# Inverse levels 2 to 16 on 32x32 diagonal tiles, with regrouped late attention halves, narrow gates and a reordered entry, pooling and head

## What is computed

```python
h = rms_norm(x, mix_norm[l]); proj = h @ w_in[l]
# A: dilated windowed attention, 4 heads x 64, rotary        (q, k, v, 256 columns each)
# B: trailing means over 2, 4, 8, 16 positions, minus itself (256 columns)
# C: gated DeltaNet, 4 heads x 128, chunks                    (q, k, v, z, and 8 gate columns)
x = x + concat(A, B, C) @ w_out[l]
```

```python
A = where(strict, (kb @ kc.T) * decay, 0)
T = triangular_solve(eye + A, eye, lower=True)     # the inverse
u = T @ vb;  w = T @ (kb * exp(g))                 # then a scan over the chunks
```

## Time and profile before

| | us |
|---|---|
| median of 3 runs | 1066.82 (1066.77 to 1066.97) |
| the profiled execution | 1069.16 |
| its span, first to last instruction | 1067.4 |

### The profile page before, as it was taken

The page is one execution under the profiler, slowest core; times in us unless marked ns, Lnnn a source line. Parts: engine busy times, 40 slices in busy tenths (PEclk is TensorE's granted clock), DMA queues, the critical chain, the costliest instruction groups (busy, mean ns, idle before and its releaser), DMA issues.

```text
span 1067.4 us, 18495 instructions
## 1 busy us (share of the span) xinstructions
PE 1040.5 (97%) x6251; PEld 905.6 (85%) x6251; DVE 743.0 (70%) x1188; ACT 608.9 (57%) x1066; POOL 228.0 (21%) x257
## 2 busy tenths in 40 slices
PE   6999999999999999999999999999999999999997
PEld 5888888999987888888888888888989778888885
DVE  5766666788856866666686666669887766666665
ACT  5655555667544655555575555557665455555554
POOL 2311111097400221111122111112004003111111
PEclk9999999999999999999999999999999999999999
DMA  8866665674113476666647666665732036666661
GB/s 262 251 198 180 196 190 167 172 204 155 60 60 99 132 220 182 195 195 181 196 129 221 182 194 195 182 195 140 197 124 95 3 117 201 194 193 191 187 196 39
DMA packets 252040, 177.97 MB, mean 167 GB/s; under 512 B 5892, under 2 KB 237593, under 8 KB 251865
## 3 DMA queue, kind: packets, MB, share of 16 engines
q1 hardware_dynamic: 250880, 175.40, 55.7%
q0 software_dynamic: 432, 1.48, 0.4%
q10 hardware_dynamic: 680, 0.46, 0.1%
HBM read 176.26 MB, written 1.05 MB: 166 GB/s over the span
## 4 chain that ended last, share of the span: by engine, by line
PE 87%; DVE 5%; ACT 4%; issue 2%; POOL 1%; DMA 1%; DVEq 0%; ACTq 0%; POOLq 0%
PE bank L679 27%; PE bank L682 14%; PE bank L661 12%; PE bank L662 12%; PE bank L663 12%; DVE Wl L1716 1%; PE bank L1028 1%; PE bank L1017 1%; ACT Wh L1279 1%; PE bank L688 1%; DVE X L1748 1%; DVE xr L1920 1%; ACT X L1345 1%; PE bank L968 1%; PE bank L919 1%
## 5 line engine op out<-in xcount | busy, mean ns | idle before, releaser
L1716 DVE TENSOR_TENSOR Wl<-raw,Wh 128x1024 fp32r<-128x1024 f32 x330 | 423.0, 1288 | 84.2 <-ACT Wh L1279 83.8
L1279 ACT ACTIVATE Wh<-raw 128x1024 fp32r<-128x1024 f32 x330 | 337.5, 1053 | 77.2 <-PE bank L663 76.8
L679 PE MATMUL bank<-X,Wh 128*128 128x512 f32 x1344 | 334.7, 391 | 0.0
L679 PEld LDWEIGHTS bank<-X,Wh 128*128 128x128 f32 x1344 | 246.7, 188 | 47.6
L576 POOL TENSOR_TENSOR gact<-gact,pooled 128x256 f32<-128x256 f32 x88 | 79.2, 900 | 613.2 <-DVE gact L1804 462.3
L682 PEld LDWEIGHTS bank<-X,Wl 128*128 128x128 f32 x1344 | 183.0, 190 | 14.0 <-DVE Wl L1716 1.2
L682 PE MATMUL bank<-X,Wl 128*128 128x256 f32 x1344 | 187.8, 283 | 0.0
L661 PE MATMUL bank<-Wh,aH 128*128 128x512 f32 x336 | 132.4, 394 | 1.4 <-DVE aL L1825 1.4
L662 PE MATMUL bank<-Wl,aH 128*128 128x512 f32 x336 | 131.8, 392 | 0.0
L663 PE MATMUL bank<-Wh,aL 128*128 128x512 f32 x336 | 130.8, 389 | 0.0
L1381 ACT ACTIVATE dec<-bank 128x256 f32<-128x256 f32 x88 | 33.6, 382 | 121.7 <-PE bank L682 121.6
(11 more groups left out here) (270 smaller groups left out, 1302.5 us busy)
## 6 DMA issues: line engine op xcount, KB each, us to landing
raw<-in_ffn_w_gate SPq DMA_DIRECT2D x88, 512.0 KB, 4.0
raw<-in_ffn_w_up SPq DMA_DIRECT2D x88, 512.0 KB, 3.7
raw<-in_ffn_w_down SPq DMA_DIRECT2D x88, 512.0 KB, 4.4
raw<-in_w_in SPq DMA_DIRECT2D x50, 512.0 KB, 4.1
raw<-in_w_out SPq DMA_DIRECT2D x16, 512.0 KB, 3.3
cst<-in_consts POOLq DMA_DIRECT2D x1, 1280.0 KB, 6.1
xr<-in_x SPq DMA_DIRECT2D x2, 512.0 KB, 4.7
out_x<-big SPq DMA_DIRECT2D x3, 256.0 KB, 2.0
```

Source lines behind the costliest of these rows:

```text
L679: nc.tensor.matmul(b[:, :], piece(Wh, s)[:, k, :], X[:, k, :, :], start=k == 0, stop=False)
L1279: return nc.scalar.activation(Wh[:, s, :], raw[:, s, :], ACT.Copy).then_inc(hi_cast.sem, 1)
L1716: return nc.vector.tensor_tensor(Wl[:, s, :], raw[:, s, :], Wh[:, s, :].bitcast(F32), ALU.subtract).then_inc(lo_cast.sem, 1)
```

## The change

The levels 2 to 16 move to compact blocks: D32 and T32 hold, for each unit, the four 32x32 diagonal blocks under one another. Each level's P and D product becomes four products per unit, one per diagonal tile, with 16 columns; masks, copies and transposes shrink to a quarter. After level 16 the compact blocks are copied into Dm and DT, which GpSimd has cleared. The late attention projections are cut into groups of four (high parts) and four (low parts) records and placed between all stages. The low casts 23 to 28 move behind the levels. The gate piece has 8 columns; its product puts the weights' high and low part side by side (16 rows) against both parts of x, and small products with a comb of ones turn and add them. copy_half(2) moves ahead of the scaled copies, which also trade places with casts 6 and 7. Pooling moves ahead of the state, scores 2 and 3 ahead of the second V products, the first Xl subtraction ahead of the second normalisation. A table load moves from ahead of the V copies to behind level 4. The norm weights come over ScalarE's queue, and at the start ScalarE casts a weight piece before the splits and squares half 1 last.

```diff
...
         X0h, X0l = X0[:, :, 0, :], X0[:, :, 1, :]
         PM = sb("PM", [P, UNITS, P])
+        D32 = sb("D32", [P, UNITS, BLOCK])
...
-        gate_cols = gact[:, 0, :]
+        gate_cols = gact[0:2 * GATES, :, :]
+        gate_raw = raw[:, MIX_SLOTS[POS_GATES], 0:KT * GATES].rearrange("p (k c) -> p k c", k=KT)
...
+                pool.wait_ge(*gates_proj.at(layer, 1))
+                nc.gpsimd.memset(Dm[0:BLOCK, :, BLOCK:HALF], 0.0)
+                nc.gpsimd.memset(DT[:, :, :], 0.0).then_inc(cleared.sem, 1)
...
                 split(POS_GATES)
                 pe.wait_ge(*att_read.at(layer, 5))
-                s = MIX_SLOTS[POS_GATES]
                 for k in range(KT):
-                    m = three(bank[1][:, 0:SEQ], piece(Wh, s)[:, k, :], piece(Wl, s)[:, k, :], X0h[:, k, :], X0l[:, k, :],
-                              k == 0, k == KT - 1)
+                    m = nc.tensor.matmul(bank[1][0:2 * GATES, :], gate_weights[:, k, :, :], X0[:, k, :, :],
...
                         for c in range(HALVES):
-                            m = nc.tensor.transpose(bank[0][:, SEQ + c * P:SEQ + (c + 1) * P],
-                                                    gate_cols[:, c * P:(c + 1) * P], ident)
+                            for i in range(2):
+                                m = nc.tensor.matmul(bank[0][:, SEQ + c * GATES:SEQ + (c + 1) * GATES],
+                                                     gate_cols[:, i, c * P:(c + 1) * P], cst[0:2 * GATES, C_GATE:C_GATE + GATES],
+                                                     start=i == 0, stop=i == 1)
                         m.then_inc(gates_in.sem, 1)
...
-                def att_late(j):
-
+                def late_of(j):
+                    c = j % 2
+                    s0, s1 = MIX_SLOTS[POS_LATE], MIX_SLOTS[POS_LATE + 1]
+                    return (bank[ATT_BANKS[j]][:, 0:2 * P].rearrange("p (s c) -> p s c", s=2),
+                            slice(c * P, (c + 1) * P), slice(s0, s1 + 1, s1 - s0))
+
+                def late_high(j, ks):
+
+                    out, t, pair = late_of(j)
+                    pe.wait_ge(*hi_cast.at(layer, MIX_BASE + POS_LATE + 2))
+                    pe.wait_ge(*z_act.at(layer, j - ATT_EARLY + 3))
+                    for k in ks:
+                        w = Wh[:, pair, k * P:(k + 1) * P]
+                        nc.tensor.matmul(out, Xh[:, k, t], w, start=k == 0, stop=False)
+                        nc.tensor.matmul(out, Xl[:, k, t], w, start=False, stop=False)
+
+                def late_low(j, ks):
+
+                    out, t, pair = late_of(j)
                     split(POS_LATE + 1)
-                    pe.wait_ge(*z_act.at(layer, j - ATT_EARLY + 3))
-                    att_part(layer, j, range(KT)).then_inc(att_in.sem, 1)
+                    for k in ks:
+                        m = nc.tensor.matmul(out, Xh[:, k, t], Wl[:, pair, k * P:(k + 1) * P], start=False, stop=k == KT - 1)
+                    return m
...
-                        even = Dm[:, u, :].rearrange("p (n a s) -> p n a s", a=2, s=LEVELS[n])[:, :, 0, :]
-                        m = nc.tensor.matmul(bank[4 + c][:, h * EVEN:(h + 1) * EVEN], LT[:, u, :], even, start=True, stop=True)
+                        for q in QUARTERS:
+                            even = D32[q, u, :].rearrange("p (n a s) -> p n a s", a=2, s=LEVELS[n])[:, :, 0, :]
+                            m = nc.tensor.matmul(bank[4 + c][q, h * EVEN:(h + 1) * EVEN], LT[q, u, q], even,
+                                                 start=True, stop=True)
...
                     for h, u in units(c):
-                        m = nc.tensor.matmul(bank[6 + c][:, h * EVEN:(h + 1) * EVEN], DT[:, u, :], PM[:, u, 0:EVEN],
-                                             start=True, stop=True)
+                        for q in QUARTERS:
+                            m = nc.tensor.matmul(bank[6 + c][q, h * EVEN:(h + 1) * EVEN], T32[q, u, :], PM[q, u, 0:EVEN],
+                                                 start=True, stop=True)
                     m.then_inc(dd_done.sem, 1)
...
+                    j, k = ATT_EARLY + n // 2, 4 * (n % 2)
                     for c in range(HALVES):
                         level_p(n, c)
+                    late_high(j, range(k, k + 2))
                     for c in range(HALVES):
                         level_d(n, c)
+                    late_high(j, range(k + 2, k + 4))
                 for c in range(HALVES):
                     quarter_p(c)
-                att_late(6)
+                late_low(6, range(0, 4))
                 for c in range(HALVES):
                     quarter_d(c)
+                late_low(6, range(4, 8)).then_inc(att_in.sem, 1)
+                for c in range(HALVES):
+                    half_p(c)
+                late_low(7, range(0, 4))
+                for c in range(HALVES):
+                    half_d(c)
+                late_low(7, range(4, 8)).then_inc(att_in.sem, 1)
                 turn_qk()
-                for c in range(HALVES):
-                    half_p(c)
-                att_late(7)
-                for c in range(HALVES):
-                    half_d(c)
...
-                m.then_inc(ks_ps.sem, 1)
-                for h in range(DN_HEADS):
-                    m = nc.tensor.matmul(bank[6][:, h * P:(h + 1) * P], QK[:, h, 0, P:SEQ], St[:, h, :], start=True, stop=True)
-                m.then_inc(qs_ps.sem, 1)
-
                 pe.wait_ge(*att_read.at(layer, 8))
                 for j in range(2):
...
+                m.then_inc(qs_ps.sem, 1)
+
+                scores(2)
+                scores(3)
+
                 pe.wait_ge(*r1_done.at(layer, 1))
                 for h in range(DN_HEADS):
...
                 if first:
-                    for c, b in ROW_ORDER:
+                    for c, b in ROW_ORDER[0:2]:
                         square(c, b)
+                    hi_first(layer, 0, 0)
                     act.wait_ge(zeroed.sem, 2)
                     act.wait_ge(*turned.at(layer, 2))
-                    split(0)
-                    split(1)
-                    hi_first(layer, 0, 0)
-                    split(2)
-                    split(3)
+                    for j in range(4):
+                        split(j)
                     hi_first(layer, 0, 1)
                 else:
                     act.wait_ge(*turned.at(layer, 4 * n + 2))
...
                 hi_mix(layer, 5)
+                copy_half(2)
+                hi_mix(layer, 6)
                 scaled_high(0)
                 scaled_high(1)
-                hi_mix(layer, 6)
+                hi_mix(layer, 7)
                 scaled_high(2)
                 scaled_high(3)
-                hi_mix(layer, 7)
-                copy_half(2)
                 copy_half(3)
                 hi_mix(layer, 8)
                 hi_mix(layer, 9)
...
                         act.wait_ge(*dd_done.at(layer, 2 * n + c + 1))
-                        src = bank[6 + c][:, 0:256].rearrange("p (u n s) -> p u n s", u=4, s=s)
-                        nc.scalar.activation(blocks(Dm, c, s)[:, :, :, 0, :], src, ACT.Copy).then_inc(d_done.sem, 1)
+                        src = bank[6 + c][:, 0:4 * EVEN].rearrange("p (u n s) -> p u n s", u=4, s=s)
+                        even = D32[:, 4 * c:4 * c + 4, :].rearrange("p u (n a s) -> p u n a s", a=2, s=s)[:, :, :, 0, :]
+                        nc.scalar.activation(even, src, ACT.Copy).then_inc(d_done.sem, 1)
                     if n == 0:
                         hi_mix(layer, 28)
-                copy_half(6)
-                for c in range(HALVES):
-                    u = slice(4 * c, 4 * c + 4)
-                    src = bank[6 + c][:, 0:P].rearrange("p (u s) -> p u s", u=4)
+                    if n == 1:
+                        act.preload_act_table_set(LN_EXP)
+                act.wait_ge(*cleared.at(layer, 1))
+                act.wait_ge(*d_done.at(layer, 8))
+                nc.scalar.activation(Dm[QUARTERS[0], :, QUARTERS[0]], D32[QUARTERS[0], :, :], ACT.Copy)
+                nc.scalar.activation(Dm[QUARTERS[1], :, QUARTERS[1]], D32[QUARTERS[1], :, :],
+                                     ACT.Copy).then_inc(dm_joined.sem, 1)
+
+                def edge(c):
+                    return slice(4 * c, 4 * c + 4), bank[6 + c][:, 0:P].rearrange("p (u s) -> p u s", u=4)
+
+                for c in range(HALVES):
...
 
             act.dma_start(cst[:, 0:C_FIRST], consts[:, 0:C_FIRST]).then_inc(consts_in.sem, 16)
+            for n, weight in enumerate((ffn1_norm, mix_norm, ffn2_norm)):
+                act.dma_start(nrm_rows[n * DEPTH * KT:(n + 1) * DEPTH * KT, :],
+                              weight.rearrange("l (k c) -> (l k) c", c=P)).then_inc(norms_in.sem, 16)
...
                 small(nc.vector.scalar_tensor_tensor(gneg[:, :, 4:8], row(1), -1.0, row(1), ALU.mult, ALU.min))
+                conv_rest(9)
...
+                dve.wait_ge(*lt_done.at(layer, 2))
+                for q in QUARTERS:
```

(22 more changed lines are left out.)

163 lines of the change are left out of this document (87 added, 76 removed).

## The result

The changed kernel takes 1070.46 us (median of 7 runs, 1069.28 to 1072.04), the kernel before 1066.90 (1066.74 to 1067.39): a ratio of 1.0037, 95% interval 1.0026 to 1.0047. It is slower by 3.6 us; 23.7 us faster was forecast. The profiled executions differ by less, 1068.4 against 1067.4 us of span, because that of the kernel before took 1069.16 us, 2.3 more than its median.

A forecast was written before the change was run, and what follows sets the result against it. TensorE, busy 97% of the span, bounds the kernel. Terms -7.7 - 15.2 - 0.4 + 1.0 + 0 - 1.3 = -23.6 us, set against the 1067.4 us span, give 1043.8, against the 1066.82 median 1043.2 us; range 1034 to 1054.

The forecast's parts named there:

- Part 2: Inverse levels 2 to 16: a group on four diagonal tiles takes 0.84 us instead of 1.79; -15.2 us over 16 groups.
- Rival A: Levels 2 to 16: issue limit, step not below 16.7 ns, group 1.38 us; 1051.8 us, chance 0.07.
- C: Levels 2 to 16, rival: tiles of one bank take turns, 33 ns a record, group 2.4 us; 1068.5 us, chance 0.03.
- Rival D: Levels: small-tile bursts with waits bring 1.2 GHz from the first level until behind level 64; +39 us, 1082, chance 0.04.
- point of decision: Levels and following stages: Rival D decides once 12 us of such work per layer run at half clock.
- Part 1: Mixer entry: 2.44 us wait and 1.5 of half clock go, new wait 1.0, gate product 0.9 less; -7.7 us.
- Part 3: Between entry and inverse: GpSimd's two memsets, about 1.5 us, delay its decay-row product; +1.0 us, layer 0 only.
- Part 4: Head: moved pooling and scores cost +0.6 us per layer, the earlier Xl subtraction gives -0.6; together 0 us.
- Part 5: Start: norm weights on ScalarE's queue shorten TensorE's 2.53 us wait, root about 1 us earlier; -1.3 us.
- Cover: Levels: late attention pieces between groups hide mask waits, 0.5 us behind about 1.0 us of work; nothing taken.

The follow-up runs named there:

- e2: Changed kernel with levels 2 to 16 on two 64x64 diagonal tiles instead of four 32x32 ones; 1055.70 us, ratio 0.9898 to the kernel before.
- e7: Kernel before with VectorE's subtraction and a further 512-column transpose ahead of each level's first mask; 1085.22 us in one run (before: 1067.06).
- e4: Kernel before with VectorE's subtraction of a weight piece moved ahead of each level's first mask; 1069.23 us in one run (before: 1065.42).
- e10: Changed kernel with 64x64 tiles, copy 4 and gates copy earlier, pool products ahead of second value product, old start; 1051.95 us, ratio 0.9866 to the kernel before.
- e5: Changed kernel with the four records of each late piece between the groups issued twice; 1075.47 us (1066.14 to 1080.35 in ten runs).
- e8: Kernel before with only copy_half(2) moved, behind the cast of piece 5 instead of piece 7; 1065.82 us, ratio 0.9989.

## Why the prediction failed, point by point

**The place.** Layer 0, from the traces: entry -1.7, levels to the first scores +2.5, head +0.7, Xl subtraction -0.6, together +0.9 us; -3.8, -7.8, +0.6 and -0.6 were forecast. This is against the profiled execution of the kernel before, which is 2.3 us above its median; against the median the loss is larger.

**Part 2, the records: right.** A group's 64 records start within 0.55 us (0.53 forecast), a step of 8.7 ns; group and piece take 1.33 (1.31). Rival A, 16.7 ns, is out, and so is C, turns within a bank: four row tiles write one bank, each its own 32 partitions of it, at 8.7 ns a record. Of the two rules of the Trainium skill that the prediction weighed, the floor of about 25 ns ("TensorE: Matmul & The Clock Gate", Back-to-back issue gap) doesn't hold for tiles in turn, and the bar on row tiles in one bank ("TensorEngine Tiling (Array Packing)", Restrictions and Gotchas) shows no cost here. At full clock the stretch from levels to scores would take e2's 301.72 - 280.12 = 21.60 us less 8 x (1.72 - 1.33), 18.5 by this estimate, 7.8 less than before. That is the forecast.

**Part 2, the step that failed.** It priced a group by its records alone, with "64 x 8.2 = 0.53 us", and nothing for how the instructions reach TensorE. The groups use them faster than blocks arrive: stops of 0.59 us and 0.34 (inside the group at 288.73, 1.39 us long instead of 1.05) in layer 0, 0.34 and 1.18 in layer 1.

**Rival D, the argument against it.** "I expect no wait over 1 us there" failed in two ways. There was one of 1.18, from a source that isn't a wait in the program. And 1 us was the wrong measure: it was taken from the 2.44 us at entry, a stage of 256-column products, while in the levels 0.60 is enough (e7). The rival itself is what happened, with two corrections: the clock fell behind the first stops and not at the first level, 6 us into the levels (7 in layer 1, in the stop of 1.18), and it cost less than +39, because records at half clock don't all take twice as long (a cycle of 2.13 against 1.33). Layer 0: 28.87 - 0.93 of stops - 18.5 = 9.4 us up to the scores, 0.5 in the head. Its point of decision, 12 us per layer at half clock, was passed (23 and 20 up to the scores). It stood at a chance of 0.04.

**Part 1, entry: half right.** The wait of 2.44 and the half clock behind it went, but the half clock wasn't there to be won in each execution. The row was read from the one of 1069.16 us, which lost the clock in both layers, and the sum was set against a median of 1066.82; e4, with the same entry, lost it in one layer. So by this difference up to 2.3 of the 3.0 us counted for the clock (1.5 a layer) were not in the median; that is an estimate. Against that one execution, the copy behind the first convolution product, ScalarE's, starts 3.65 us earlier though the stage began 0.3 later: 3.95 against a forecast of 3.8. The gate product waits 0.90 (1.0) and takes 1.87 us (1.89). Not seen: VectorE's copy of the gates stands behind five subtractions, 7.99 us for the five, so that TensorE waits 0.96 ahead of the next product but one. And the four small gate products, priced at "nothing (0 to +0.4)", hold up the records around them by 1.17 us, where the two transposes did by 0.22: 0.95. They are eight records a layer as against two, not four: the transposes have one record each. That leaves 2.0; measured are 1.7 a layer (1.9 in layer 1), and 0.3 I didn't trace. e10 took the two waits away.

```profile
219.94 2.02 PE L821 MATMUL bank<-X,Wh 128*16 128x512 f32 x8 [0.90 <-ACT big L1549]
...
217.06 7.99 DVE L1777 TENSOR_TENSOR Wl<-raw,Wh 128x1024 fp32r<-128x1024 f32 x5
224.97 0.67 DVE L2038 TENSOR_TENSOR gact<-bank,pooled 16x512 f32<-16x512 f32 x1
```

**Part 3, GpSimd: right in mechanism.** The clearings take 0.30 + 0.94 us (1.5 forecast). No wait shows in the changed kernel, since TensorE came 1.5 us earlier and not 3.8; in e10, where it did, the wait was 1.5, and moving the clearings gave the 1.3 expected.

**Part 4, head: right.** The wait ahead of o_ps 2 is 0.93 (1.2 to 1.5), the subtraction gave 0.6 (0.6). Of the 0.7 us lost up to it, 0.5 is clock.

**Part 5, start: wrong in sign.** The wait for the norm weights is 0.6 us shorter (1.91 against 2.53), but the first down product begins 0.3 later: half of the squares now end last, and the root waits for them.

**Cover.** No wait of TensorE for a mask shows in the levels.

## To carry to other kernels

Splitting products into small tiles multiplies instructions: count them per microsecond as well as their columns, and compare with the closest blocks on the instruction queue (here one of about 250 in 3.4 to 4.7 us, up to 6.0 when weights move). Judge a new stall in a stage by what a stall of that size did in that same stage, and in more than one layer or run: 0.60 us in the levels cost some 7 us a layer (e7 against e4, one run each: 18.2 less 3.8, halved), 0.96 us among 256-column products only itself, and 1.84 to 2.44 us there sometimes the clock and sometimes not. Before a wait's half clock is counted as a gain, see whether the median has it, and not only the profiled execution. A middle tile size, less tight in instructions, can beat the smallest even with slower records.

## What the runs showed of the hardware

- TensorE can stop inside a run of products with no semaphore involved: 0.2 to 1.7 us, by the count and the dates of the packets at the end of a block of about 250 instructions. In the profile this is "issue" inside a group, at the same record in kernels whose instructions up to there are the same.
- The clock fell with TensorE 98% busy over the run, behind single stops of 0.59 and 0.60 us in the inverse, with TensorE at work again at once. It stayed at 0.50 for 3.4 us (layer 1 of e5) to 24 us (layer 0 of the changed kernel).
- At the mixer's entry the same wait of 2.4 us lost the clock in one layer and kept it in the other (e4), and so did one of 1.8 (e8).
- Four 32x32 tiles in turn: 8.7 ns a record at full clock. Two 64x64 tiles with 32 columns, or two of 32x32 with 64 columns: some 30 ns.
- Open: why blocks come no closer, why moving weights delay them, and what beside a stop's length decides whether the clock falls: the levels are more sensitive than the entry, and at the entry the outcome varies.
